# A 22nd weight slot in the routing's temporaries, and who waits for the first gather

## The chip, the cores and the metric

The kernel runs on one core of a Trainium2 chip. The metric is the device time of one execution in microseconds (us), less is better. "SP" is the engine that issues the weight loads, "POOL" is GpSimd, which issues gathers and scatters, "PE" is TensorE, "DVE" is VectorE and "ACT" is ScalarE. All of them run their own instruction streams and meet in semaphores.

## The reference, cut to what matters

The kernel computes one step of a two-layer encoder trunk on 512 prompt rows and 32 sample rows of 1024 floats. Each layer is an attention mixer followed by a mixture of experts (MoE) with 4 groups of 8 experts; a row goes to the two best experts of its best group:

```python
g_idx = jnp.argmax(pg, axis=-1)
...
top_v, top_i = lax.top_k(pe, TOP_K_IN_GROUP)
...
for g in range(N_GROUPS):
    a = jnp.einsum('nd,edf->nef', x, w_gate[g])
    u = jnp.einsum('nd,edf->nef', x, w_up[g])
    hh = jax.nn.silu(a) * u * gate[:, g, :, None].astype(x.dtype)
    y = y + jnp.einsum('nef,efd->nd', hh, w_down[g])
```

Each of the 32 experts has a gate, an up (1024 x 256) and a down matrix (256 x 1024), 1 MB each in float32, so a layer reads 96 MB of expert weights.

## The kernel before, in words

Attention and its projections run first. While the last output projections run, the rows are normed, turned, and routed: `logits`, `route_pick` and `route_place` find for each row its two experts and its place in them; `route_slots` multiplies a selection matrix (`sel`) with one-hot rows (`hot2`) and so makes, in PSUM, the list of rows of each expert. From it DVE makes the indices `idx_i` (L1425 to L1432), and POOL gathers the rows of two experts at a time from `hn_scratch` into `xg` (`gather`, L669). The rows are turned by `x_turn` (L2060).

Then 32 experts follow in order. For each: `gate_up` (L2075, L2076, 16 matmuls), ACT's SiLU (L966), DVE's product (L1475), `h_transpose` (L2082), `down` (L2087, L2088), DVE's copy (L1490), POOL's `scatter` to `y_scratch` (L675). TensorE does `gate_up(e)`, then `x_turn` after an odd e, `down(e - 1)`, `h_transpose(e)`. An expert has room for 64 rows. If one has more (`extra > 0`), an "overfull" expert is computed with the rest: picked after `OV_PICK`, listed after `OV_LIST`, its rows gathered by POOL at `OV_GATHER = 18`, and computed after expert `OV_AFTER` (L2125 turns its rows). With these inputs that happens once, in layer 1.

SP issues all weight loads in one order (`READ_ORDER`: gate and up of an expert, then down of the one before). They go round a ring of slots, `MOE_SLOTS`, of 2048 floats by 128 partitions. Six slots are the ring of the attention weights, the others are lent by tiles whose contents are over at some time; `vacant` says for what SP has to wait before a lent slot is first used in a layer. X0 and X1 lie in the turned rows of the routing, and H1 and H0 in `hid` itself, whose rows are read back from `hn_scratch` after the last use of each (L552). From the second turn on a load waits for the last use of the slot's former matrix (`load_after_owner`). The ring's slots R4, R5 and S0 are left out for one turn (`LEFT_OUT`) and take the three matrices of the overfull expert, which SP issues just before the load of `(OV_AFTER, 2)`.

Before H1, SP waits until the first gather of the layer has landed:

```python
if name == "H1":
    sp.wait_ge(gath[0], 16 * (TWOS // XG * layer + 1))
```

SP is in order, so H0 and all later loads are behind that wait.

After the last expert the rows are read back from `y_scratch`, weighted and added to `hid` (`combine`), and layer 1 or the final norm follows.

Of the kernel before, what the change touches and what calls it, by code (L numbers as in the profile page):

```python
# [21 lines left out]
ALU = mybir.AluOpType  # L22
# [3 lines left out]
D = 1024  # L26
SEQ, DEC, PAST = 512, 32, 256
CHUNK, WINDOW = 64, 128
N = SEQ + DEC
P = 128  # L30
KD = D // P
NT = 5
# [16 lines left out]
G, EPG, F = 4, 8, 256  # L49
NE = G * EPG  # L50
CAP = 64
MAX_EXTRA = 17
KEY0 = 2048
OUT_HALF = D // 2

SLOT = 2048
XG = 2
TWOS = NE // 2
OV_AFTER = 20
OV_PICK, OV_LIST, OV_GATHER = 14, 16, 18  # L60
assert OV_AFTER % 2 == OV_PICK % 2 == OV_LIST % 2 == 0

# [2 lines left out]
NL = 40  # L65
L_E = 8

UNITS = NT * 4
# [112 lines left out]

A_RING = ["R0", "R1", "R2", "R3", "R4", "R5"]
B_RING = ["R0", "R1", "R2", "R3", "R4", "R5"]
MOE_SLOTS = [["N0", "R4", "R5", "S0", "N1", "F5", "F6", "F0", "F1", "F2", "F3", "F4", "W0", "R0", "R1", "R2", "R3", "X0", "X1", "H1", "H0"]] * 2
NSLOT = len(MOE_SLOTS[0])


# [38 lines left out]
def program(nc, ctx, I, O):  # L226
# [3 lines left out]
    def sem(name):  # L230
        return ctx.enter_context(nc.semaphore(name))
# [6 lines left out]
    cst = sb("cst", [P, C_END])  # L238
# [5 lines left out]
    M0 = 7296  # L244
# [9 lines left out]
    def part(at, *shape):  # L254
        n = int(np.prod(shape))
        v = area[:, at:at + n]
        if len(shape) == 2:
            v = v.rearrange("p (a b) -> p a b", b=shape[1])
        if len(shape) == 3:
            v = v.rearrange("p (a b c) -> p a b c", b=shape[1], c=shape[2])  # L260
        return v

    slot_at = {f"R{i}": R_R + SLOT * i for i in range(6)}
    slot_at.update({f"F{i}": R_F + SLOT * i for i in range(7)})
    slot_at["S0"], slot_at["W0"] = R_S, 4864
    slot_at.update({f"N{i}": R_N + SLOT * i for i in range(2)})
    slot_at.update({f"X{i}": R_X + SLOT * i for i in range(2)})

# [55 lines left out]
    assert M1 + 1792 + 2 * 512 <= slot_at["W0"] and slot_at["W0"] + SLOT <= M0  # L324
    ovw = part(R_R + 4 * SLOT, 3, SLOT)
    y2b = [part(2 * D * i, 2, D) for i in range(3)] + [part(R_X + 2 * D * i, 2, D) for i in range(2)]
    assert 6 * D <= M0 and 4 * D <= KD * N


    stage_g, stage_e = part(M0, 2, KD, G), part(M0 + 64, 2, KD, NE)  # L330
    lg = part(M0, NT, NL)
    em = part(M0 + 200, NT, NE)

    hot2 = [part(M0 + 360 + 320 * i, NT, 2 * NE) for i in range(2)]
    hot = [h[:, :, 0:NE] for h in hot2]
    both = part(M0 + 1000, NT, NE)
    sofar = part(M0 + 1160, NT, NE)
    blocks = part(M0 + 1000, NE * 8)
    sel = [part(M0 + 1320 + 640 * i, NT, P) for i in range(2)]
    gtop, etop = part(M0 + 2600, NT, 8), part(M0 + 2640, NT, 8)  # L340
    chosen = part(M0 + 2680, NT, 4)
    where = part(M0 + 2700, NT, 2)
    pen = part(M0 + 2710, NT, G)
    rs = part(M0 + 2730, 12, 8)
    gexp = part(M0 + 2826, NT, G)
    gw = part(M0 + 2846, 2, 8)
    ovs = part(M0 + 2862, 128)
    shifted = part(M0 + 2990, NT, 2)
    root = part(M0 + 3000, NE)
    assert M0 + 3000 + NE <= R_G  # L350
    first_of = sb("first_of", [P, NT, 2, 8], U32)
    idx_i = sb("idx_i", [P, 3, NE], I32)
    ov_i = sb("ov_i", [P, 8], I32)
# [49 lines left out]
        sem("r_mm"), sem("r_exp"), sem("r_hot"), sem("r_before"), sem("r_sel"), sem("r_slots"), sem("r_idx"))  # L403
    r_d, r_sum = sem("r_d"), sem("r_sum")
    r_clear = sem("r_clear")
    ones = cst[:, C_ONE:C_ONE + P]
    before = cst[:, C_BEFORE:C_BEFORE + P]
    slot_no = cst[:, C_SLOT:C_SLOT + CAP].unsqueeze(1).broadcast_to([P, 2, CAP])
# [13 lines left out]
    def wait_apart(eng, s, value):  # L422

        eng.wait_ge(s, value)
        eng.sem_inc(passed, 1)
# [18 lines left out]
    def vacant(layer, name):  # L444

        c = "ab"[layer]
        if name in ("F5", "F6"):
            return [(pos_mm, len(POS))] if layer else [(q_mm, 16), (kv_mm, NT)]
        if layer and name in ("F0", "F1", "F2"):
            return [(at["b", "pv"], 15), (vb_out[0], 64)]  # L450
        if name[0] == "F":
            return [(at[c, "o"], UNITS)] + ([(vb_out[1], 64)] if layer else [(k_out, 16 * 6)])
        if name[0] == "N":
            return [(kb_out[0], 64), (kb_out[1], 64), (pos_mm, len(POS)), (made_once, 2)] if layer else [(y_flip, NT)]
        if name == "W0":
            return [(at[c, "o"], UNITS)]
        if name[0] == "X":
            return [(r_mm, NT * (layer + 1))]
        if name[0] == "H":
            return [(y_flip, NT * (2 * layer + 2)), (sumsq, NT * (2 * layer + 2))] + \  # L460
                [(y_out[b], 16 * (3, 2)[b] * (layer + 1)) for b in range(2)]
        return None
# [27 lines left out]
    def _(sp):  # L490
# [29 lines left out]
        def moe_loads(layer):  # L520
            s = ov[layer]

            def overfull_weights(o):
                wait_apart(sp, s["pick"], o + 1)
                e = sp.value_load(ov_u[0:1, 0:1], min_val=0, max_val=NE - 1)
                for j, w in enumerate((gate, up, down)):
                    src = w[layer][bass.ds(e, 1)].rearrange("o p k f -> p (o k) f")
                    sp.dma_start(ovw[:, j, :].rearrange("p (k f) -> p k f", f=src.shape[-1]), src) \
                      .then_inc(s["w"], 16)

            for n, (key, name) in enumerate(MOE_LOADS[layer]):
                if key[2:] == (OV_AFTER, 2):
                    for j in range(3):
                        sp.wait_ge(*last_use(("e", layer, *READ_ORDER[LEFT_OUT + j - NSLOT])))
                    sp.wait_ge(s["count"], layer + 1)
                    extra = sp.value_load(ov_i[0:1, layer:layer + 1], min_val=0, max_val=MAX_EXTRA)
                    with sp.If(extra > 0):
                        overfull_weights(0)
                free = vacant(layer, name) if expert_stream(*key[2:]) < NSLOT else None
                if free is None:  # L540
                    load_after_owner(key)
                else:
                    for signal in free:
                        sp.wait_ge(*signal)
                    if name == "H1":
                        sp.wait_ge(gath[0], 16 * (TWOS // XG * layer + 1))
                    load(key)

            for name in ("H1", "H0"):
                sp.wait_ge(*last_use([key for key, at in MOE_LOADS[layer] if at == name][-1]))  # L550
                for t in (2 * int(name[1]), 2 * int(name[1]) + 1):
                    sp.dma_start(hid[:, t, :], hn_dram[COL[t]:COL[t] + P, :]).then_inc(tile_in[t], 16)  # L552

            with sp.If(extra > 1):
                with sp.Fori(1, extra) as o:
                    overfull_weights(o)
# [29 lines left out]
    def _(pool):  # L586
# [77 lines left out]
        def moe(layer):  # L664
# [27 lines left out]
            for b in range(2):  # L692
                pool.wait_ge(y_out[b], 16 * (3, 2)[b] * (layer + 1))
            wait_apart(pool, r_idx, 2 * layer + 1)
            for j in range(XG):
                gather(j)
            pool.wait_ge(r_idx, 2 * layer + 2)
            for e in range(NE):
# [428 lines left out]
    def _(dve):  # L1127
# [175 lines left out]
        def moe(layer):  # L1303
# [122 lines left out]
            for b in range(2):  # L1426
# [1 line left out]
                ins = nc.vector.tensor_scalar(idx_i[rows, 1, 0:TWOS], idx_i[rows, 2, :].rearrange("p (j b) -> p b j", b=2)[:, b, :],  # L1428
                                              1, None, ALU.arith_shift_right)
            ins.then_inc(r_idx, 1)  # L1430
            own(dve, nc.vector.tensor_scalar(em[:, 0, :], ps[:, 3, 0:NE], -2.0, float(2 * KEY0), ALU.mult, ALU.add))
            nc.vector.tensor_scalar(idx_i[:, 0, :], em[:, 0, :], cst[:, C_HALF:C_HALF + 1], None, ALU.add) \  # L1432
                .then_inc(r_idx, 1)

            def per_tile(i):
# [78 lines left out]
            def overfull_select(o):  # L1514

                dve.wait_ge(s["mask"], o + 1)
                ins = nc.vector.tensor_copy(blocks[:, 0:NE], ps[:, 3, 0:NE])
                nc.vector.tensor_scalar(shifted[:, :, :], where[:, :, :], ps[:, 3, 64:65], None, ALU.subtract) \
                    .then_inc(s["seen"], 1)
                wait_apart(dve, s["seen"], o + 1)  # L1520
                for t in range(NT):
                    r = ROWS[t]
                    for c in range(2):
                        ins = nc.vector.tensor_scalar(sel[c][:r, t, :].rearrange("p (a b) -> p a b", b=CAP), slot_no[:r], shifted[:r, t, c:c + 1],
                                                      cst[:r, (C_K1, C_K2)[c] + t:(C_K1, C_K2)[c] + t + 1],
                                                      ALU.is_equal, ALU.mult)
                ins.then_inc(s["list"], 1)
# [51 lines left out]
            with dve.If(extra > 1):  # L1579
                with dve.Fori(1, extra) as o:  # L1580
                    overfull_pick(o)
                    overfull_select(o)
                    wait_apart(dve, s["scat"], 16 * o)
                    overfull_rows(o)
                    overfull_expert(o)

# [144 lines left out]
    def _(pe):  # L1731
# [316 lines left out]
        def moe(layer):  # L2048
# [63 lines left out]
            def overfull_list(o):  # L2112
                pe.wait_ge(s["list"], o + 1)
                for t in range(NT):
                    r = ROWS[t]
                    for c in range(2):
                        ins = nc.tensor.matmul(ps[:, 3, 0:2 * NE], sel[c][:r, t, :], hot2[c][:r, t, :],
                                               start=t == 0 and c == 0, stop=t == NT - 1 and c == 1)
                ins.then_inc(s["irow"], 1)

# [243 lines left out]
```

## Time and profile before

| | |
|---|---|
| three runs | 1138.3, 1138.5, 1140.09 us |
| profiled execution, its own time | 1136.48 us |
| its span in the trace | 1134.6 us |
| PE busy | 1009.6 us (89%) |
| DVE, ACT, POOL busy | 421.5, 231.9, 254.0 us |
| HBM read, over the span | 268.66 MB |
| the chain that ended last | PE 77%, DMA 13%, DVE 4% |
| weights' queue (q1) | 240.40 MB, 53.9% of the DMA engines' span |

The MoE of layer 0 runs from about 257 to 482 us, that of layer 1 from about 870 to 1104 us. The span is counted from the first instruction; the execution's own time also holds what lies around it. A busy PE is not PE at its peak, since matmuls are pipelined.

### The profile page before, as it was taken

What the parts mean: (1) busy time and instruction counts of PE and PEld (TensorE: products, weight loads), DVE (VectorE), ACT (ScalarE), POOL (GpSimd) and SP (SyncE); (2) the same over time, 40 slices, a digit from 0 to 9 for tenths busy, and PEclk for the clock granted to TensorE, in tenths of its full rate; (3) what the DMA queues carried; (4) which work ended last, traced back from release to release, by engine and by line L of the source; (5) the groups of instructions that cost most, each with busy time, mean ns of one, the idle gap of its engine ahead of it and who ended that gap; (6) DMA issues with size and microseconds to landing.
All of it is one profiled execution on the core that took longest, in us unless ns stands there. A gap on an engine that the chain in (4) does not pass through costs nothing.

```text
span 1134.6 us, 17373 instructions
## 1 busy us (share of the span) xinstructions
PE 1009.6 (89%) x6608; PEld 715.2 (63%) x6608; DVE 421.5 (37%) x1367; ACT 231.9 (20%) x717; POOL 254.0 (22%) x408
## 2 busy tenths in 40 slices
PE   6999999978999989839899899999996999888980
PEld 5877777965555545438668687777895555555540
DVE  1234454342333322241242433435464333432326
ACT  4234442110000000033222332332311000000002
POOL 3612232011222221122121221212211122221223
PEclk9999999978999999969999999999996999999995
DMA  9412141569999999993320402227066999999996
GB/s 314 124 40 75 39 186 64 217 244 336 416 419 417 416 420 418 392 317 126 119 80 27 134 31 94 66 102 290 24 258 237 382 419 417 418 418 419 418 372 243
DMA packets 73333, 282.12 MB, mean 249 GB/s; under 512 B 10410, under 2 KB 37114, under 8 KB 47200
## 3 DMA queue, kind: packets, MB, share of 16 engines
q1 hardware_dynamic: 57520, 240.40, 53.9%
q0 software_dynamic: 14480, 31.65, 8.0%
q10 hardware_dynamic: 1248, 8.91, 2.0%
q8 instruction: 56, 0.92, 0.3%
q14 instruction: 29, 0.24, 0.1%
HBM read 268.66 MB, written 28.70 MB: 262 GB/s over the span
## 4 chain that ended last, share of the span: by engine, by line
PE 77%; DMA 13%; DVE 4%; issue 2%; ACT 2%; POOL 1%; SPq 1%; POOLq 0%; ACTq 0%; DVEq 0%
PE ps L1773 22%; PE ps L2075 16%; PE ps L1765 11%; DMA area<-in_w_up 8%; PE ps L2087 7%; PE ps L2060 2%; PE ps L2266 2%; PE ps L1749 2%; PE ps L2082 2%; PE ps L1836 2%; PE ps L1958 1%; PE ps L2232 1%; PE ps L1973 1%; PE ps L1988 1%; DMA area<-y_scratch 1%
## 5 line engine op out<-in xcount | busy, mean ns | idle before, releaser
L1773 PE MATMUL ps<-area 128*128 128x256 f32 x1152 | 266.4, 384 | 7.1 <-DMA area<-in_w_b_qkv 3.3
L2076 PE MATMUL ps<-area 128*64 128x256 f32 x1040 | 251.8, 398 | 0.0
L1773 PEld LDWEIGHTS ps<-area 128*128 128x128 f32 x1152 | 214.0, 191 | 37.9 <-issue 8.2
L2075 PE MATMUL ps<-area 128*64 128x256 f32 x912 | 220.7, 397 | 14.7 <-DMA area<-in_w_up 7.7
L2075 PEld LDWEIGHTS ps<-area 128*64 128x64 f32 x912 | 125.5, 143 | 80.2 <-issue 21.1
L2076 PEld LDWEIGHTS ps<-area 128*64 128x64 f32 x1040 | 143.0, 143 | 0.0
L675 POOL DMA_INDIRECT y_scratch<-area,idx_i x64 | 63.8, 997 | 352.2 <-DVE area L1490 302.3
L1765 PE MATMUL ps<-area 128*128 128x272 f32 x512 | 123.2, 395 | 0.0
L1475 DVE SCALAR_TENSOR_TENSOR area<-ps,area 64x256 f32<-64x256 f32 x64 | 31.4, 491 | 232.4 <-ACT area L966 232.4
L966 ACT ACTIVATE area<-ps,area 64x256 f32<-64x256 f32 x64 | 29.9, 468 | 412.5 <-PE ps L2076 412.5
L2087 PE MATMUL ps<-area 128*64 128x512 f32 x228 | 108.7, 599 | 1.1 <-DVE area L1483 0.8
L2088 PE MATMUL ps<-area 128*64 128x512 f32 x228 | 108.7, 599 | 0.0
L1765 PEld LDWEIGHTS ps<-area 128*128 128x128 f32 x512 | 95.0, 190 | 18.9 <-issue 0.6
L931 ACT ACTIVATE area<-area,small 128x256 f32<-128x256 f32 (+5 forms) x160 | 80.2, 502 | 87.1 <-DVE small L1232 87.1
L1225 DVE CUSTOM_DVE_ANT_0 area<-ps,area 128x256 f32<-128x256 f32 (+5 forms) x160 | 59.1, 423 | 44.9 <-PE ps L1958 25.2
L793 POOL TENSOR_SCALAR area<-area,small 32x288 f32<-32x288 f32 (+4 forms) x40 | 20.5, 521 | 162.1 <-DVE small L1661 162.1
L2082 PEld LDWEIGHTS ps<-cst,area 64*128 64x128 f32 x130 | 20.2, 203 | 55.1 <-issue 53.6
L2087 PEld LDWEIGHTS ps<-area 128*64 128x64 f32 x228 | 28.7, 136 | 41.0 <-issue 32.4
L660 POOL TENSOR_SCALAR area<-area,small 128x256 f32<-128x256 f32 (+2 forms) x80 | 33.7, 439 | 92.5 <-DVE small L1260 92.5
L1470 DVE TENSOR_TENSOR area<-ps,gT 128x512 f32<-128x512 f32 x65 | 44.9, 691 | 13.8 <-PE ps L2060 7.6
L2060 PE MATMUL ps<-cst,area 128*128 128x128 f32 x256 | 38.7, 296 | 11.7 <-DMA area<-hn_scratch,idx_i 11.7
L2060 PEld LDWEIGHTS ps<-cst,area 128*128 128x128 f32 x256 | 32.3, 196 | 23.6 <-issue 17.7
(235 smaller groups left out, 1163.6 us busy)
## 6 DMA issues: line engine op xcount, KB each, us to landing
area<-in_w_up SPq DMA_DIRECT2D x65, 1024.0 KB, 24.6
area<-in_w_gate SPq DMA_DIRECT2D x57, 1024.0 KB, 23.0
area<-in_w_down SPq DMA_DIRECT2D x57, 1024.0 KB, 27.4
area<-in_w_b_qkv SPq DMA_DIRECT2D x12, 1024.0 KB, 8.5
hid<-in_w_down SPq DMA_DIRECT2D x8, 1024.0 KB, 24.5
hid<-in_w_gate SPq DMA_DIRECT2D x8, 1024.0 KB, 20.8
area<-y_scratch ACTq DMA_DIRECT2D x8, 1024.0 KB, 8.1
area<-in_w_a_qkv SPq DMA_DIRECT2D x6, 1024.0 KB, 13.0
```

Source lines behind the costliest of these rows:

```text
L675: nc.gpsimd.indirect_dma_start(y2_dram, bass.IndirectOffsetOnAxis(ap=idx_i[:, 0, e:e + 1], axis=0), yout[e % 2], None, bounds_check=4 * N ...
L931: ins = nc.scalar.activation(E[:r, g, 0:nk], E[:r, g, 0:nk], ACT.Exp, bias=sm[:r, 4 + g:5 + g], scale=SCALE, accum_out=sm[:r, 8 + g:9 + g])
L1225: ins = nc.vector.tensor_tensor_reduce(out=E[:r, g, 0:nk], in0=ps[:r, b, c:c + nk], in1=tab(j, g)[:r, tc:tc + nk], scale=1.0, scalar=-3e38 ...
L1470: return nc.vector.tensor_tensor(x, turned, gT[:, layer, :].unsqueeze(2).broadcast_to([P, KD, CAP]), ALU.mult)
L1765: ins = nc.tensor.matmul(ps[:, bank, 0:HALF_N], w[:, k, m * P:m * P + P], x[:, k, HALF_N * h:HALF_N * h + HALF_N], start=k == 0, stop=k == ...
L1773: ins = nc.tensor.matmul(ps[:r, bank, at_col:at_col + F], x[:, k, COL[t]:COL[t] + r], w[:, k, :], start=k == k0, stop=k == k1 - 1)
L2060: ins = nc.tensor.transpose(ps[:, 2 + k // 4, k % 4 * P:k % 4 * P + P], x[:, k, :], ident)
L2075: nc.tensor.matmul(ps[0:CAP, bank, 0:F], x[:, k, :], wg[:, k, :], start=k == 0, stop=k == KD - 1)
L2076: ins = nc.tensor.matmul(ps[CAP:P, bank, 0:F], x[:, k, :], wu[:, k, :], start=k == 0, stop=k == KD - 1)
L2082: ins = nc.tensor.transpose(ps[:, bank, c * CAP:c * CAP + CAP], rows[:, c, :], ident[CAP:P, CAP:P])
L2087: nc.tensor.matmul(ps[0:CAP, bank, :], ht[:, c, :], wd[:, c, 0:OUT_HALF], start=c == 0, stop=c == 1)
L2088: ins = nc.tensor.matmul(ps[CAP:P, bank, :], ht[:, c, :], wd[:, c, OUT_HALF:D], start=c == 0, stop=c == 1)
```

## The change

The routing's temporaries, which filled one stretch from M0 on, are laid out anew: those that are dead once the row lists stand in PSUM (`sel`, `both`, `sofar`, `em`) lie together, and a slot M of 2048 floats at 6960 covers them. The others (`hot2`, `lg`, `gtop`, `root`, ...) lie behind it; `idx_f` takes the place of `em` for the scatter's indices, `blocks` goes to the end of the turned rows' region, and the selection of the overfull expert gets tiles of its own (`ov_sel`). The ring has 22 slots, in another order: N1, F5 and F6 come before R4, R5, S0, and M stands between H1 and H0. `OV_AFTER` is 22, which keeps the left-out turn on R4, R5 and S0.

H1 waits no longer for the first gather. M waits for the last attention output, for the row lists (`r_slots`) and for a new semaphore `asked`, which POOL raises when it has issued gather 0. H0 is behind M in SP's order.

```diff
-OV_AFTER = 20
+OV_AFTER = 22
...
-MOE_SLOTS = [["N0", "R4", "R5", "S0", "N1", "F5", "F6", "F0", "F1", "F2", "F3", "F4", "W0", "R0", "R1", "R2", "R3", "X0", "X1", "H1", "H0"]] * 2
+MOE_SLOTS = [["N0", "N1", "F5", "F6", "R4", "R5", "S0", "F0", "F1", "F2", "F3", "F4", "W0", "R0", "R1", "R2", "R3", "X0", "X1", "H1", "M", "H0"]] * 2
...
-    slot_at["S0"], slot_at["W0"] = R_S, 4864
+    slot_at["S0"], slot_at["W0"], slot_at["M"] = R_S, 4864, 6960
...
+    R_T = 7232
+    sel = [part(R_T + 640 * i, NT, P) for i in range(2)]
+    both, sofar, em = (part(R_T + 1280 + 160 * i, NT, NE) for i in range(3))
+    stage_g, stage_e = part(R_T, 2, KD, G), part(R_T + 64, 2, KD, NE)
+    R_P = slot_at["M"] + SLOT
...
+    hot2 = [part(R_P + 320 * i, NT, 2 * NE) for i in range(2)]
...
+    idx_f = part(R_P + 1272, NE)
+    blocks = part(R_X + 2 * SLOT, NE * 8)
...
+    ov_at = [R_G + P * i for i in range(8)] + [R_F + 7 * SLOT + P * i for i in range(2)]
+    ov_sel = [[part(ov_at[NT * c + t], P) for t in range(NT)] for c in range(2)]
...
+    asked = sem("asked")
...
+        if name == "M":
+            return [(at[c, "o"], UNITS), (r_slots, layer + 1)]
...
-                    if name == "H1":
-                        sp.wait_ge(gath[0], 16 * (TWOS // XG * layer + 1))
+                    if name == "M":
+                        sp.wait_ge(asked, layer + 1)
                     load(key)
...
-            for j in range(XG):
+            gather(0)
+            pool.sem_inc(asked, 1)
+            for j in range(1, XG):
                 gather(j)
...
-            own(dve, nc.vector.tensor_scalar(em[:, 0, :], ps[:, 3, 0:NE], -2.0, float(2 * KEY0), ALU.mult, ALU.add))
-            nc.vector.tensor_scalar(idx_i[:, 0, :], em[:, 0, :], cst[:, C_HALF:C_HALF + 1], None, ALU.add) \
+            own(dve, nc.vector.tensor_scalar(idx_f, ps[:, 3, 0:NE], -2.0, float(2 * KEY0), ALU.mult, ALU.add))
+            nc.vector.tensor_scalar(idx_i[:, 0, :], idx_f, cst[:, C_HALF:C_HALF + 1], None, ALU.add) \
                 .then_inc(r_idx, 1)
...
-                        ins = nc.vector.tensor_scalar(sel[c][:r, t, :].rearrange("p (a b) -> p a b", b=CAP), slot_no[:r], shifted[:r, t, c:c + 1],
+                        ins = nc.vector.tensor_scalar(ov_sel[c][t][:r, :].rearrange("p (a b) -> p a b", b=CAP), slot_no[:r], shifted[:r, t, c:c + 1],
...
-                        ins = nc.tensor.matmul(ps[:, 3, 0:2 * NE], sel[c][:r, t, :], hot2[c][:r, t, :],
+                        ins = nc.tensor.matmul(ps[:, 3, 0:2 * NE], ov_sel[c][t][:r, :], hot2[c][:r, t, :],
```

## Rows read from the trace of the kernel before

**Rows 1.** Waits of TensorE, 257 to 480 us: us in total, times, longest

```profile
PE ps L2075 <- DMA area<-in_w_up: 10.2, 7, 2.5
PE ps L2060 <- DMA area<-hn_scratch,idx_i: 5.7, 1, 5.7
```

**Rows 2.** ScalarE's timeline, layer 0: SiLU of experts 0, 22 and 31 (start, us)

```profile
265.53 0.47 ACT L966 ACTIVATE area<-ps,area 64x256 f32<-64x256 f32 x1 [10.81 <-PE ps L2076]
...
404.92 0.47 ACT L966 ACTIVATE area<-ps,area 64x256 f32<-64x256 f32 x1 [6.47 <-PE ps L2076]
...
476.74 0.47 ACT L966 ACTIVATE area<-ps,area 64x256 f32<-64x256 f32 x1 [6.51 <-PE ps L2076]
```

**Rows 3.** TensorE's timeline: start, us; in brackets idle before it and releaser

```profile
473.02 0.40 PE L2075 MATMUL ps<-area 128*64 128x256 f32 x1 [1.22 <-DMA area<-in_w_up]
...
1018.89 1.06 PE L2125 MATMUL ps<-cst,area 64*128 64x64 f32 x8 [2.26 <-DMA area<-hn_scratch,ov_i]
...
1020.74 0.43 PE L2075 MATMUL ps<-area 128*64 128x256 f32 x1 [0.78 <-DVE area L1470]
...
1094.50 0.43 PE L2075 MATMUL ps<-area 128*64 128x256 f32 x1
```

**Rows 4.** Windows: PE, PEld, DVE, ACT, POOL busy; then PEclk, DMA share, GB/s

```profile
252.00:253.00 1.00, 0.00 (x0) 0.00 (x0) 0.89 (x8) 0.00 (x0) 0.00 (x0) 0.50 0.00 0
...
866.00:867.00 1.00, 0.00 (x0) 0.00 (x0) 0.87 (x6) 1.00 (x1) 1.00 (x1) 0.50 0.08 33
...
265.00:472.00 207.00, 195.95 (x1388) 111.87 (x1384) 62.76 (x122) 14.49 (x31) 42.58 (x42) 0.98 1.01 412
879.00:1090.00 211.00, 200.06 (x1426) 114.03 (x1426) 69.06 (x152) 14.49 (x31) 43.55 (x43) 0.98 1.01 413
...
257.00:263.00 6.00, 4.86 (x22) 3.29 (x24) 0.69 (x1) 0.00 (x0) 1.00 (x1) 0.50 0.86 308
870.00:878.00 8.00, 7.14 (x34) 4.44 (x36) 0.69 (x1) 0.00 (x0) 0.99 (x1) 0.50 0.83 317
```

**Rows 5.** Waits of SP's queue, whole span: us in total, times, longest

```profile
SPq L546 <- DMA area<-hn_scratch,idx_i: 20.9, 2, 11.2
```

**Rows 6.** SP's timeline: the issue of H1 in layer 0 and in layer 1

```profile
257.33 0.33 SPq L513 DMA_DIRECT2D hid<-in_w_down  x1
...
869.96 0.33 SPq L513 DMA_DIRECT2D hid<-in_w_down  x1
```

**Rows 7.** Single transfers: gathers of 253.3, 260.1, 283.3 and 296.1; load of 245.2

```profile
L669 POOL DMA_INDIRECT area<-hn_scratch,idx_i x1: 1312/1312/1312, 253.3 to 253.3; - x1
...
DMA to landing us min/median/max: 4.0/4.0/4.0
...
L669 POOL DMA_INDIRECT area<-hn_scratch,idx_i x1: 1002/1002/1002, 260.1 to 260.1; - x1
...
DMA to landing us min/median/max: 6.2/6.2/6.2
...
L669 POOL DMA_INDIRECT area<-hn_scratch,idx_i x2: 1048/1050/1052, 283.3 to 296.1; - x2
...
DMA to landing us min/median/max: 9.3/9.3/9.3
...
L513 SPq DMA_DIRECT2D area<-in_w_gate x1: 328/328/328, 245.2 to 245.2; - x1
...
DMA to landing us min/median/max: 5.0/5.0/5.0
```

**Rows 8.** Line L528: loads of the overfull expert, issue ns, start, us to landing

```profile
L528 SPq DMA_DIRECT2D area<-in_w_down x1: 2327/2327/2327, 981.0 to 981.0; - x1
...
DMA to landing us min/median/max: 26.5/28.8/29.3
```

**Rows 9.** Line L513, 1064.5 to 1065: the last up matrix of layer 1

```profile
L513 SPq DMA_DIRECT2D area<-in_w_up x1: 2642/2642/2642, 1064.5 to 1064.5; - x1
...
DMA to landing us min/median/max: 28.8/28.8/28.8
```

## What the change is expected to do

> **What bounds the kernel now.** I read the waits of TensorE first, then ScalarE's timeline (its one SiLU for each expert, L966, follows that expert's gate and up matmuls, so it is a clock of the experts), then the busy shares of the DMA engines, then the two DMA queues around the start of each MoE stage, because the change touches only what is loaded there.
>
> In the MoE stage of layer 0 TensorE sets the pace at first: the SiLU of expert 0 starts at 265.53 and that of expert 22 at 404.92 [rows 2], 139.39 / 22 = 6.34 us an expert. At that pace expert 31 would come at 404.92 + 9 x 6.34 = 462.0. It comes at 476.74 [rows 2], 14.7 us later. The reader is to see why: TensorE waits for an up matrix seven times [rows 1], and the last expert starts at 473.02 when its own up matrix lands [rows 3]. From 265 to 472 the DMA engines are full, share 1.01 at 412 GB/s [rows 4]. So the end of layer 0's MoE is the end of a stream of bytes that runs without a gap from about 265; TensorE falls into it near expert 23.
>
> In layer 1 the engines are as full (1.01 at 413 GB/s [rows 4]), but TensorE loses time on an overfull expert, which is computed after expert 20, and so is never caught by the weights. The margin at the end is thin: the last up matrix is issued at 1064.51 and takes 28.8 us [rows 9], so it is there at 1093.3, and expert 31 starts at 1094.50 [rows 3], 1.2 us later. Inside the overfull expert TensorE stands 2.26 us for the gather of its rows [rows 3]. So layer 1 is bound by TensorE's own order plus that wait, with the stream right behind.
>
> Ahead of both stages there is a hole in the DMA time. SP holds H1 back until the first gather has landed; the two waits sum to 20.9 us, the longer 11.2 [rows 5], so the other is 9.7. H1 is issued at 257.33 and at 869.96 [rows 6]; without the wait it would go at 257.33 - 9.7 = 247.6 and 869.96 - 11.2 = 858.8. From 252 to 253 the engines move nothing, and from 866 to 867 their share is 0.08 [rows 4].
>
> **The change, part by part.**
>
> *A 22nd slot.* Each layer loads 96 matrices of 1.05 MB (128 x 2048 floats). Those that find a lent slot free go before expert 0 is done; the rest are in the saturated stream. With 22 slots 74 are left for it in place of 75. H1 moves into the hole, M takes H1's place behind it. One load less is 1.05 MB / 412 GB/s = 2.55 us [rows 4]. In layer 0 that goes whole into the end, since the last up matrix releases the last expert: -2.55. It is far from being used up: the lateness there is 14.7 us. In layer 1 nobody waits for the stream, so by itself it is worth nothing and adds 2.55 to the margin of 1.2.
>
> *The overfull expert after expert 22 and not 20.* Its own work and its DMAs stay as many; its place in the streams of TensorE, ScalarE, VectorE and POOL is two experts later, 2 x 6.34 = 12.7 us. The gather of its rows keeps its place at expert 18. It lands at 1018.89 at the latest [rows 3], and is now wanted at about 1018.89 - 2.26 + 12.7 = 1029.3. So the wait goes: -2.26 in layer 1, nothing in layer 0, where this work is not entered. What is late next? Its three matrices. They now stand in SP's order before load 70 and not before load 64, so six more loads are ahead of them and, by the 22nd slot, one less: 5 x 2.55 = 12.8 us later. The third one is issued at 980.96 and the three take up to 29.3 us [rows 8], so it lands by 1010.3; it would land by 1023.1. TensorE wanted them at 1020.74 [rows 3] and will at 1020.74 - 2.26 + 12.7 = 1031.2. Eight us are over. Before these loads SP now waits for expert 17's gate matmuls, with everything in SP's queue behind it; that is some 7 us of waiting, while the loads already issued cover 28.8 us [rows 9]. So no engine runs dry. Then TensorE's gain of 2.26 has to fit the stream: 1.2 + 2.55 - 2.26 leaves 1.5 us. It fits.
>
> *H1 earlier.* Its bytes follow X1's in the same queue. In layer 0 they are through well before the gather at 253.3 brings its first ones. In layer 1 it is closer: H1 leaves at 858.8 behind X0 and X1, the engines are nearly idle from 866 on [rows 4], and 2.55 us more end at 868.5 at the latest, a us or so before the gather that H1 used to wait for landed, at about 869.9 [rows 6]. So it can run beside that gather's first bytes; this is in the bounds below.
>
> *M behind the first gather, not behind its landing.* POOL spends 1.31 us on the gather that starts at 253.3 and it lands after 4.0 [rows 7]. `asked` comes with the end of that instruction, so M leaves at about 254.7, H0 right behind. A lone 1.05 MB load takes 5.0 us to land [rows 7], of which its bytes are 2.55; so M's bytes cannot be there much before the gather's last ones. The first gather of each layer is on the path: TensorE stood 5.7 us for it [rows 1], and every us it lands later is a us on both the start of TensorE and the start of the stream. No row has a first gather beside a load, so bounds: below, 0; above, 2.2 a layer, because the gather of 260.1, issued with H1 and H0 in flight, takes 6.2 against 4.0 [rows 7]; farther still 5.3, because in the full stream a gather takes 9.3 [rows 7]. I take 0.3 a layer, near the lower end, as M starts 1.4 us behind. A gain is excluded, since before the gather had the engines to itself.
>
> By the row of 260.1 a load beside a gather costs that gather 2.2 us. The Trainium skill's page "DMA: Bandwidth & Descriptors", section "Queues, rings and completion order", says each DMA engine takes turns, a packet at a time, between the queues that have work, so SP's weights would not wait behind POOL's gather but take every other turn. That speaks against lending the engines to M before the gather is in; by it, with full overlap, the gather's half MB would take twice its 1.3 us, and the sum below would come to -2.3. The rows of 4.0 and 6.2 agree with it in kind.
>
> *The rest.* The temporaries at new addresses, the separate list tiles for the overfull expert, `idx_f`: the same instructions with the same shapes, 0. One semaphore increment on POOL between gathers 0 and 1, whose second is wanted ten us later, and one more wait on SP: 0. The lent slots H1 and H0 are used one expert longer, so the reload of `hid` waits one expert longer; its packets are behind some 28 us of issued loads and stay there: 0. The new order of the first slots moves loads that end long before they are read: 0.
>
> **The sum** against the profiled execution's 1136.48 us (span 1134.6): -2.55 - 2.26 + 0.3 + 0.3 = -4.2, so 1132.3. The median of the runs is 2.0 higher, at 1138.5; with the same difference, 1134.3.
>
> One more term has a width and no sign: TensorE's granted clock is 0.50, that is 1.2 GHz, from 257 to 263 in layer 0 and from 870 to 878 in layer 1 [rows 4], after it stood for the gather. The two stretches differ by 2 us, worth 1 us of work at half rate. A shifted start may land on either: up to 1 us each way and layer.
>
> **The rivals.** A change within 0.2% (2.3 us) is about what a measurement of this kernel can't tell from none.
>
> 1. *The forecast*, -4.2: 1134.3, own range 1132.7 to 1135.9 (on one side -4.8 with both gathers undisturbed and a us of clock; on the other half of the 2.2 a layer). Chance 0.68.
> 2. *The gathers share with the weights in full*, 2.2 each: -4.8 + 4.4 = -0.4, 1138.1. For it is the gather of 260.1; against it the head start of 1.4 us. Chance 0.13.
> 3. *A wait in the place of the removed one in layer 1* (the overfull expert's matrices or the stream): only layer 0 gains, -2.55 + 0.3 = -2.25, 1136.2. Against it are the 8 us and the 1.5 us above. Chance 0.09.
> 4. *Slower*: H1's tail, M and H0 together treat the first gather as the full stream treats any, 9.3 in place of 4.0: -4.8 + 10.6 = +5.8, 1144.3. It decides from 2.4 us of delay a layer. Against it, at 254.7 only one load's bytes can be near. Chance 0.06.
> 5. *The slot does nothing*, because slots and not bytes limit layer 0's stream: the overfull term and the delays stay, -2.26 + 0.6 = -1.7, 1136.8. The share of 1.01 speaks against it. Chance 0.04.
>
> Faster by over 0.2%: case 1 nearly whole and half of case 3, 0.71. Within: case 2, the other half of 3, case 5, and a little of 1, 0.21. Slower: case 4 and the clock's bad side on case 2, 0.08. The range runs from the forecast's low end with a second us of clock to case 2 with one on its bad side, and leaves out case 4: 1131.5 to 1139.0.
>
> **What the profile after would show.** H1's issue near 247.6 and 858.8 minus the shift; M's some 1.4 us after the gather's start. First gathers landing after 4.0 to 4.6 us: above 6 is case 2 or 4. The last up matrix of layer 0, counted from expert 0's SiLU, 2.55 us sooner, with TensorE still waiting there. No wait at L2125 before the overfull expert, and none for its weights. If expert 31 in layer 1 waits for `in_w_up`, the margin was wrong. What would make the total wrong: a late first gather, or a longer stretch at the low clock in either stage.

## The result and the profile after

The changed kernel takes 1147.65 us (median of four runs, 1147.15 to 1149.63), the kernel before 1138.56 beside it; the ratio is 1.0075, 95% interval 1.0054 to 1.0096. It is 9.1 us slower where 4.2 less was forecast. The profiled execution took 1147.15 us, its span is 1145.3, against 1136.48 and 1134.6 before.

TensorE's waits in the changed kernel, first from 250 to 500 us, then from 860 to 1130 us (us in total, times, longest; line 2070 was 2060, 2085 was 2075):

```profile
PE ps L2070 <- DMA area<-hn_scratch,idx_i: 12.4, 1, 12.4
PE ps L2085 <- DMA area<-in_w_up: 8.8, 5, 2.8
...
PE ps L2070 <- DMA area<-hn_scratch,idx_i: 11.1, 1, 11.1
```

The wait for the first gather was 5.7 us in layer 0 [rows 1] and 6.0 in layer 1; it is 12.4 and 11.1 now. The gather itself shows why. Its own line in each layer, and how long it took to land:

```profile
L677 POOL DMA_INDIRECT area<-hn_scratch,idx_i x1: 1313/1313/1313, 252.9 to 252.9; - x1
...
DMA to landing us min/median/max: 10.6/10.6/10.6
...
L677 POOL DMA_INDIRECT area<-hn_scratch,idx_i x1: 1395/1395/1395, 869.8 to 869.8; - x1
...
DMA to landing us min/median/max: 9.3/9.3/9.3
```

It lands after 10.6 and 9.3 us; before it was 4.0 [rows 7] and, in layer 1, 4.2. And the timeline of all engines around it, in layer 0:

```profile
252.72 0.33 SPq L521 DMA_DIRECT2D area<-in_w_gate  x1
...
252.86 1.31 POOL L677 DMA_INDIRECT area<-hn_scratch,idx_i  x1 [9.82 <-DVE idx_i L1442]
...
253.22 0.33 SPq L521 DMA_DIRECT2D hid<-in_w_up  x1
```

SP issues M at 252.72, that is 0.14 us *before* POOL's engine begins the gather, and H0 at 253.22, while the engine is still at work on it (1.31 us). The forecast had M at 1.4 us behind the gather's start. So 2.1 MB of weights are in the queues before the gather's first row is. H1, now free, is not out of the way either: issued at 246.05, it lands 9.3 us later, 2.5 us after the gather's start, and the DMA engines stand at a share of 0.99 where they moved nothing before [rows 4]:

```profile
252.00:253.00 1.00, 0.00 (x0) 0.00 (x0) 0.91 (x6) 0.32 (x2) 0.14 (x1) 0.50 0.99 418
```

ScalarE's SiLUs, the clock of the experts (experts 0, 22, 31 of layer 0, then 0, 22, the overfull one, 23 and 31 of layer 1):

```profile
272.42 0.47 ACT L976 ACTIVATE area<-ps,area 64x256 f32<-64x256 f32 x1 [18.13 <-PE ps L2086]
...
411.85 0.47 ACT L976 ACTIVATE area<-ps,area 64x256 f32<-64x256 f32 x1 [6.47 <-PE ps L2086]
...
480.56 0.47 ACT L976 ACTIVATE area<-ps,area 64x256 f32<-64x256 f32 x1 [6.20 <-PE ps L2086]
...
887.46 0.47 ACT L976 ACTIVATE area<-ps,area 64x256 f32<-64x256 f32 x1 [16.20 <-PE ps L2086]
...
1035.23 0.47 ACT L976 ACTIVATE area<-ps,area 64x256 f32<-64x256 f32 x1 [6.47 <-PE ps L2086]
1046.85 0.47 ACT L981 ACTIVATE area<-ps,area 64x256 f32<-64x256 f32 x1 [11.15 <-PE ps L2086]
1058.41 0.47 ACT L976 ACTIVATE area<-ps,area 64x256 f32<-64x256 f32 x1 [11.10 <-PE ps L2086]
...
1108.99 0.47 ACT L976 ACTIVATE area<-ps,area 64x256 f32<-64x256 f32 x1 [5.23 <-PE ps L2086]
```

This gives the ledger. Expert 0 of layer 0 is 6.89 us later than at 265.53 [rows 2]. From expert 0 to 31 it takes 208.14 us, 3.07 less than before (476.74 - 265.53 = 211.21 [rows 2]). From there to expert 0 of layer 1 it takes 406.90 against 402.32 (expert 0 of layer 1 was at 879.06 before): 4.58 more, of which the second late gather is 5.1. Inside layer 1 it takes 221.53 against 219.16, 2.37 more; that was forecast as 2.26 less. The end is 0.07 shorter. 6.89 - 3.07 + 4.58 + 2.37 - 0.07 = 10.7, the difference of the spans. Against the forecast's -4.2 that is 14.9 us too much: 11.1 for the two gathers (11.7 measured, 0.6 forecast) and 5.0 for the step around the overfull expert, treated next; the slot gave 0.5 more than forecast, and all the rest took 0.7 less.

The loss inside layer 1 is in the step around the overfull expert: 23.18 us from expert 22 to 23 (1035.23 to 1058.41). Before it was 20.43, from expert 20 (1014.58) to 21 (1035.01). The windows of the changed kernel there (sixth column PEclk, the granted share of TensorE's clock):

```profile
1041.00:1044.00 3.00, 3.00 (x16) 1.66 (x14) 0.00 (x0) 0.00 (x0) 0.39 (x1) 0.50 0.99 414
...
1047.00:1050.00 3.00, 1.63 (x8) 0.67 (x10) 0.78 (x2) 0.32 (x1) 0.00 (x0) 0.90 1.00 410
1050.00:1052.00 2.00, 1.91 (x6) 0.23 (x2) 0.05 (x1) 0.00 (x0) 0.00 (x0) 0.50 1.04 434
...
1054.00:1056.00 2.00, 2.00 (x12) 1.23 (x10) 0.00 (x0) 0.00 (x0) 0.00 (x0) 0.50 1.02 426
```

and the same part in the kernel before:

```profile
1021.00:1024.00 3.00, 3.00 (x18) 1.72 (x16) 0.00 (x0) 0.00 (x0) 0.00 (x0) 0.55 1.02 423
1024.00:1027.00 3.00, 2.10 (x16) 1.05 (x12) 0.29 (x1) 0.47 (x1) 0.00 (x0) 0.88 1.03 410
1027.00:1031.00 4.00, 2.36 (x10) 0.80 (x10) 1.18 (x3) 0.00 (x0) 0.00 (x0) 1.00 1.02 422
```

The reader is to see one short fall to 1.2 GHz before, and two long ones after. In windows of 1 us the granted clock is at 0.50 for some 3.4 us from 1021.3 on before, and for some 6.8 us each from 1039.4 and from 1049.4 on after; each fall comes behind a stretch in which TensorE stood part of the time.

The wait at L2135 (L2125 before) for the overfull expert's gather is gone, as forecast. But TensorE still stands there, for DVE's copy of the expert before:

```profile
1038.35 1.11 PE L2135 MATMUL ps<-cst,area 64*128 64x64 f32 x8 [1.07 <-DVE area L1500]
```

This wait of 1.07 us was there before as well, hidden under the one of 2.26: TensorE stood from 1016.63 (1018.89 - 2.26) and DVE's copy ended at 1017.56. So the move could give 2.26 - 1.07 = 1.2 us and not 2.26. Two things were to be tested: what the early loads cost, and what the clock does.

### The profile page after: what moved, and what is told of

Read it like the earlier page. It is cut to its first block, busy times and chain, and to the rows that moved or that the text cites. A ratio compares the mean times of both kernels' runs of the same rounds, so it can differ in the third digit from the quotient of the medians.

```text
span 1145.3 us, 17377 instructions
## 1 busy us (share of the span) xinstructions
PE 1010.7 (88%) x6608; PEld 714.2 (62%) x6608; DVE 421.8 (37%) x1367; ACT 231.9 (20%) x717; POOL 254.4 (22%) x408
## 4 chain that ended last, share of the span: by engine, by line
PE 81%; DMA 10%; DVE 4%; issue 2%; ACT 2%; POOL 1%; SPq 0%; ACTq 0%; POOLq 0%; DVEq 0%
PE ps L1783 22%; PE ps L2085 18%; PE ps L1775 10%; PE ps L2097 9%; DMA area<-in_w_up 5%; PE ps L2070 3%; PE ps L2276 2%; PE ps L2092 2%; DMA area<-hn_scratch,idx_i 2%; PE ps L1759 2%; PE ps L1846 1%; PE ps L1968 1%; PE ps L2242 1%; PE ps L1983 1%; PE ps L1998 1%
## 5 line engine op out<-in xcount | busy, mean ns | idle before, releaser
L2085 PE MATMUL ps<-area 128*64 128x256 f32 x976 | 237.5, 399 | 17.2 <-DMA area<-in_w_up 8.8
L2086 PE MATMUL ps<-area 128*64 128x256 f32 x944 | 230.3, 400 | 0.0
L2085 PEld LDWEIGHTS ps<-area 128*64 128x64 f32 x976 | 135.0, 143 | 89.9 <-issue 26.7
L2097 PE MATMUL ps<-area 128*64 128x512 f32 x236 | 113.7, 604 | 1.1 <-DVE area L1493 0.8
L2098 PE MATMUL ps<-area 128*64 128x512 f32 x236 | 113.6, 604 | 0.0
```

What stands on the lines that cost most here:

```text
L2085: nc.tensor.matmul(ps[0:CAP, bank, 0:F], x[:, k, :], wg[:, k, :], start=k == 0, stop=k == KD - 1)
L2086: ins = nc.tensor.matmul(ps[CAP:P, bank, 0:F], x[:, k, :], wu[:, k, :], start=k == 0, stop=k == KD - 1)
L2097: nc.tensor.matmul(ps[0:CAP, bank, :], ht[:, c, :], wd[:, c, 0:OUT_HALF], start=c == 0, stop=c == 1)
L2098: ins = nc.tensor.matmul(ps[CAP:P, bank, :], ht[:, c, :], wd[:, c, OUT_HALF:D], start=c == 0, stop=c == 1)
```

## The experiments

**1 to 4. Order against place.** Each differs by a few lines from the changed kernel, the second from the one before. The cuts show the lines on which each rests. Kernel 2 also gets the increment of `asked` behind gather 0; in 1, 6, 7 and 9 to 12 nobody waits for `asked`, and the increment is taken out.

```diff
 # 1: m_after_landing (the changed kernel, M and H0 behind the landing)
-                        sp.wait_ge(asked, layer + 1)
+                        sp.wait_ge(gath[0], 16 * (TWOS // XG * layer + 1))
 # 2: before_with_asked (the kernel before, H1 and H0 wait for asked)
-                        sp.wait_ge(gath[0], 16 * (TWOS // XG * layer + 1))
+                        sp.wait_ge(asked, layer + 1)
 # 3: asked_by_engine (the changed kernel)
-            pool.sem_inc(asked, 1)
+            nc.gpsimd.memset(small[:, 52:53], 0.0).then_inc(asked, 1)
 # 4: h0_after_landing (the changed kernel)
+                    if name == "H0":
+                        sp.wait_ge(gath[0], 16 * (TWOS // XG * layer + 1))
```

> The changed kernel, but M (and H0 behind it) waits until the first gather has landed, as H1 did before. Theory A (in the changed kernel the loads of M and H0 are issued before POOL's engine has begun the gather, so their bytes are ahead of it): the first gathers land 4.0 to 4.3 us after their start again, expert 0's SiLU comes at about 265 in layer 0, and what the extra slot and the later overfull expert bring is seen: about 1134 to 1137 us, under the kernel before. Theory B (the new ring or the overfull expert's new place costs the time): first gathers as fast as before, but the time stays over 1140.

> The kernel before with one thing changed: H1, and H0 behind it, waits for the new semaphore that POOL raises behind gather 0, not for its landing. 21 slots, overfull expert after expert 20. Theory A: first gathers land after 9 to 11 us, TensorE's wait for them grows by 5 to 7 us in each layer, and nothing gives it back but the DMA time gained in layer 0: 1146 to 1151 us. Theory B: no change, 1138 to 1140.

> The changed kernel, but the semaphore is raised by a tiny memset on POOL's engine behind gather 0, which can start only when the engine has built the gather's descriptors (1.3 to 1.4 us). Theory A, order is what matters: M is issued about 1.5 us after the gather's start, the first gathers land after 4.0 to 4.6, total 1134 to 1137. Theory C, sharing is what matters, whatever the order: the first gathers land after 6 us or more, total 1138 to 1142.

> The changed kernel, but H0 waits for the landing of the first gather, so one load (M) is issued ahead of it and not two. Theory A: each load ahead costs the gather its 2.5 us of bytes, so it lands after about 7 to 8 us in place of 10.6 and 9.3: total about 1141 to 1144. Theory C with equal turns from the start of the gather: one load in place of two makes little difference while it lasts, 9 to 10 us and about 1147.

Measured, each against runs of the kernel before on the same chip; "first gathers" is the landing time in layer 0 and 1, "layer 0" from SiLU 0 to 31 in the profiled execution, "overfull step" the distance of the two SiLUs around it. The last three columns come from one profiled execution of each kernel:

| kernel | ratio to before, 95% interval | first gathers | layer 0 | overfull step |
|---|---|---|---|---|
| before | 1 | 4.0, 4.2 | 211.2 | 20.4 |
| changed | 1.0075, 1.0054 to 1.0096 | 10.6, 9.3 | 208.1 | 23.2 |
| 1, M and H0 after landing | 0.9986, 0.9969 to 1.0002 | 4.0, 5.8 | 208.4 | 23.2 |
| 2, before with `asked` | 1.0060, 1.0042 to 1.0079 | 8.3, 8.4 | 211.6 | 20.6 |
| 3, `asked` by the engine | 1.0002, 0.9980 to 1.0024 | 4.1, 8.6 | 208.3 | 23.2 |
| 4, H0 after landing | 1.0041, 1.0022 to 1.0060 | 5.6, 8.0 | 208.4 | 19.0 |

Kernel 2 has neither the new slot nor the moved expert, and loses 0.6% by the semaphore alone: theory A in kind, theory B falls. Kernel 1 undoes the early loads and is back at the time of before. In layer 0 more bytes ahead mean a later gather: 4.0 us with no early load, 5.6 with one behind H1, 8.3 with two (kernel 2, whose H1 is one of the two), 10.6 with two behind H1. In kernel 2 the DMA engines moved nothing from 253 to 254; in the changed kernel H1's last bytes were still going, which accounts in kind for 10.6 in place of 8.3. Kernel 3 splits the two theories by layer. In layer 0 it is enough that M comes behind the gather's start, here 1.5 us behind, at 254.79; the gather is in after 4.1 us:

```profile
253.27 1.31 POOL L677 DMA_INDIRECT area<-hn_scratch,idx_i  x1 [9.47 <-DVE idx_i L1442]
254.59 0.12 POOL L704 MEMSET small<- 128x1 f32 x1
254.79 0.33 SPq L521 DMA_DIRECT2D area<-in_w_gate  x1
```

The DMA engines were full of H1 when this gather began, but had room again before M came:

```profile
253.00:254.00 1.00, 0.00 (x0) 0.00 (x0) 0.90 (x5) 0.90 (x3) 0.73 (x1) 0.50 1.03 426
254.00:255.00 1.00, 0.00 (x0) 0.00 (x0) 0.87 (x6) 0.70 (x1) 0.81 (x3) 0.50 0.53 221
```

In layer 1 that is not enough: M comes as late (866.41 against 864.81), yet the gather takes 8.6 us. H1 is still on its way there: it lands 3.7 us after the gather's start (3.1 in layer 0), and the share is 0.98 from 864 to 866 and 0.83 from 866 to 868. H1 alone (kernels 1, 11 and 8) makes it 5.8, 5.0 and 5.2, where it lands 4.8, 4.1 and 3.9 us after the gather's start; in layer 0 (kernels 1, 3, 6, 8 and 11) it lands after 2.2 to 3.9 us and the gather after 3.8 to 4.6, the later the later. So theory C holds in layer 1: there the gather pays also for what comes behind it. That H1's remainder is what makes the difference between the layers is read from these rows; no run varied it alone. Kernel 4's gather of layer 0 is faster than expected, 5.6 for 7 to 8 us, and its median 1144.6 where 1141 to 1144 was expected. The totals of 1 and 3 missed their expectation, 1134 to 1137 us: they were 1138.0 and 1140.4 beside 1140.0 of before. The step around the overfull expert accounts for part of it, and H1 for another, as the next runs show.

**5 to 8. The parts one by one.**

```diff
 # 5: overfull_later_alone (the kernel before, 21 slots)
-OV_AFTER = 20
+OV_AFTER = 22
-MOE_SLOTS = [["N0", "R4", "R5", "S0", "N1", "F5", "F6", "F0", "F1", "F2", "F3", ...
+MOE_SLOTS = [["N0", "N1", "F5", "F6", "F0", "F1", "F2", "R4", "R5", "S0", "F3", ...
 # 6: m_both_h1_layer0 (the changed kernel)
-                    if name == "M":
-                        sp.wait_ge(asked, layer + 1)
+                    if name == ("M", "H1")[layer]:
+                        sp.wait_ge(gath[0], 16 * (TWOS // XG * layer + 1))
 # 7: slot_alone_h1_waits (the changed kernel)
-                    if name == "M":
-                        sp.wait_ge(asked, layer + 1)
+                    if name == "H1":
+                        sp.wait_ge(gath[0], 16 * (TWOS // XG * layer + 1))
 # 8: h1_free_alone (the kernel before)
-                    if name == "H1":
+                    if name == "H0":
```

> The kernel before with only the overfull expert moved behind expert 22 (21 slots; R4, R5 and S0 stand eighth to tenth in the ring so that the left-out turn fits). The prediction's step: its wait of 2.26 us for its gather is gone, the step around it takes 18.2 us and the kernel about 2.3 us less than before. Theory D, from the runs so far (23.2 us around it in three traces with it behind expert 22, 19.0 in one, 20.4 and 20.6 behind expert 20): without that wait TensorE's granted clock falls for longer inside it, 23 us around it and the kernel 2 to 3 us slower than before. Theory E: where the clock falls is chance, so the median is between the two.

> The changed kernel, but M waits for the first gather's landing in layer 0 and H1 does so in layer 1 (so H1 uses the idle DMA time in layer 0 alone). Theory A with what the earlier run showed of H1's tail beside layer 1's gather: first gathers land after 4.0 and 4.2 us, layer 0 from expert 0 to 31 takes 208.3 us (211.2 before), 1.6 us less than with H1 free in both. Kernel 1 to 3 us under before.

> The changed kernel with H1 waiting for the first gather's landing in both layers, as before; M and H0 behind it. The prediction's step says the slot gives 2.55 us because H1 moves into idle DMA time; with H1, M and H0 all behind the landing there are three loads in front of the ring's first refill, so layer 0 from expert 0 to 31 takes 210 to 211 us, 1 us or less under before. If it takes 208.3, the slot gives its time without the hole.

> The kernel before with the wait for the first gather moved from H1 to H0, nothing else (21 slots). Theory A: layer 0's gather still 4.0 us, layer 1's 5 to 6 us because H1's bytes are still going; layer 0's stream gains at most the 1 us in which the engines stood still before the first refill. Total 0 to 1.5 us over before.

| kernel | ratio to before, 95% interval | first gathers | layer 0 | overfull step |
|---|---|---|---|---|
| 5, overfull later alone | 0.9982, 0.9964 to 1.0000 | 4.1, 4.4 | 213.2 | 19.1 |
| 6, H1 free in layer 0 | 0.9946, 0.9928 to 0.9963 | 4.6, 4.4 | 211.4 | 19.1 |
| 7, H1, M, H0 after landing | 0.9955, 0.9936 to 0.9974 | 3.8, 4.1 | 208.7 | 19.0 |
| 8, H1 free alone | 0.9994, 0.9976 to 1.0013 | 3.8, 5.2 | 212.9 | 22.2 |

Kernel 7 is the changed one with the old wait, and is 0.45% *faster* than the kernel before; my expectation that the slot would then bring 1 us or less was wrong. Layer 0 takes 208.7, so the slot gives its time without the idle stretch ahead of the gather. There is room behind it, as the same kernel run again (12, below) shows. The first two rows are kernel 12, the third is the kernel before:

```profile
262.00:266.00 4.00, 4.00 (x22) 2.30 (x20) 0.00 (x0) 0.00 (x0) 0.00 (x0) 0.50 1.01 420
266.00:270.00 4.00, 2.62 (x24) 1.50 (x22) 1.38 (x3) 0.47 (x1) 0.00 (x0) 0.99 0.86 334
...
265.00:270.00 5.00, 3.63 (x34) 2.17 (x32) 1.38 (x3) 0.47 (x1) 0.00 (x0) 1.00 0.75 255
```

Kernel 12 has 0.90 from 265 to 270, and 0.99 from 264 to 266 where the kernel before has 0.47.

H1, M and H0, 2.5 us each from some 2 us after 257.4, are nearly done when expert 0 opens the ring's first refill at 266.8. Kernel 8 says the same from the other side: H1 in the idle stretch brings nothing by itself and makes layer 1's gather take 5.2. Kernel 5 has the forecast direction, 0.18% where 2.3 us (0.20%) was forecast, at the edge of what its interval can tell.

Kernel 6 missed its expectation twice: layer 0 took 211.4 and not 208.3, and yet it is 5.6 us under before where 1 to 3 was expected. Its trace is not typical: the profiled execution took 1138.52, one of four at 1137.3 to 1138.7, while the other eight lie at 1131.9 to 1134.0. Its layer 0 is long although its overfull step is short, so the two vary apart. Over all fourteen traces experts 0 to 22 of layer 0 take 139.4 us, whatever the kernel; the differences arise between expert 22 and 31, where TensorE waits for the weights: 71.8 to 73.7 us with 21 slots (four traces), 68.7 to 69.8 with 22 (nine traces), and 72.0 in kernel 6. That is about 3 us for the slot with a scatter of 1 to 2, and why kernel 6's trace stands out was not tried.

**9 to 12. Why the overfull step is 19 or 23 us.** Kernels 9 and 10 are kernel 7 with layer 1's first gather held back by 8 or 16 tiny memsets on POOL; 11 is kernel 1 and 12 is kernel 7 again.

```diff
             wait_apart(pool, r_idx, 2 * layer + 1)
+            for _ in range(8 * layer):
+                own(pool, nc.gpsimd.memset(small[:, 52:53], 0.0))
             gather(0)
```

> The 22-slot kernel with H1, M and H0 behind the landing (the fastest kind so far), and 8 tiny memsets on POOL before layer 1's first gather, so that layer 1's experts start about 1.7 us later, as late as with H1 free, but with no load beside the gather. Theory F (how long the granted clock stays low around the overfull expert depends on when TensorE starts, not on what the loads do): the step from expert 22 to 23 takes 23.2 us in some runs and the median is more than 1.7 us over the same kernel without the memsets, up to 1.7 + 4. Theory G (the loads beside it matter): 19.0 us around it as in the kernel without them, median 1.7 us over.

> The same with 16 memsets, about 3.4 us later. Theory F: again other than the plain 3.4 us over, by up to 4 us either way. Theory G: 3.4 us over and 19.0 us around the overfull expert.

> The changed kernel with M and H0 behind the landing and H1 free in both layers, a second time, beside the one with H1 waiting too. If the first measurement holds, it is 3 to 5 us over that one: 1.6 of it the later gather of layer 1, the rest a 23.2 us step around the overfull expert in place of 19.0 in most runs.

> The 22-slot kernel with H1, M and H0 behind the landing in both layers, a second time: 0.4 to 0.5% under the kernel before, first gathers 3.8 to 4.2 us, 19.0 us around the overfull expert.

The first gathers of the two layers take 4.0 and 4.0 us in kernel 9, 4.1 and 4.2 in 10, 4.4 and 5.0 in 11, 4.0 and 4.2 in 12.

| kernel | median, us (before: 1139.59) | ratio to before, 95% interval | overfull step |
|---|---|---|---|
| 9, 8 memsets | 1138.19 | 0.9983, 0.9966 to 1.0000 | 23.2 |
| 10, 16 memsets | 1137.59 | 0.9975, 0.9955 to 0.9994 | 19.2 |
| 11, M and H0 after landing | 1137.31 | 0.9976, 0.9957 to 0.9995 | 23.2 |
| 12, H1, M, H0 after landing | 1133.46 | 0.9948, 0.9932 to 0.9964 | 19.1 |

The memsets were cheaper than I had reckoned, 1.7 and 3.4 us: TensorE waits for layer 1's first gather for 7.04 us in kernel 9 and 8.67 in kernel 10, against 5.96 in kernel 12 and 5.92 in 7, so its start is 1.1 and 2.7 us later. (Counted from the start of the span the first `x_turn` of kernel 9 is only half a us behind kernel 12's, 869.22 against 868.69, since everything ahead of it happened to be earlier in that execution.) In kernel 9 the profiled step grew from 19.1 to 23.2 and the median by 4.7 for 1.1 us of delay. No load is beside the gather in either. So theory F says it rightly for kernel 9 and G, with 19.0 us and 1.7 over, does not. Kernel 10 does not tell them apart: its step is 19.2 and its median 4.1 over kernel 12, where G had 3.4 and F up to 4 us to either side of that. Kernel 11 is 3.9 over kernel 12, as expected. The SiLUs of kernel 9 (expert 22, the overfull one, 23), then of kernel 12:

```profile
1025.73 0.47 ACT L977 ACTIVATE area<-ps,area 64x256 f32<-64x256 f32 x1 [6.47 <-PE ps L2087]
1037.41 0.47 ACT L982 ACTIVATE area<-ps,area 64x256 f32<-64x256 f32 x1 [11.21 <-PE ps L2087]
1048.97 0.47 ACT L977 ACTIVATE area<-ps,area 64x256 f32<-64x256 f32 x1 [11.09 <-PE ps L2087]
```

```profile
1026.19 0.47 ACT L975 ACTIVATE area<-ps,area 64x256 f32<-64x256 f32 x1 [6.47 <-PE ps L2085]
1036.36 0.47 ACT L980 ACTIVATE area<-ps,area 64x256 f32<-64x256 f32 x1 [9.70 <-PE ps L2085]
1045.29 0.47 ACT L975 ACTIVATE area<-ps,area 64x256 f32<-64x256 f32 x1 [8.47 <-PE ps L2085]
```

and their windows, kernel 9 then 12:

```profile
1029.00:1037.00 8.00, 7.22 (x40) 4.24 (x40) 0.69 (x1) 0.00 (x0) 2.04 (x2) 0.57 1.02 422
...
1039.00:1046.00 7.00, 5.31 (x20) 2.10 (x22) 0.98 (x2) 0.00 (x0) 0.00 (x0) 0.58 1.01 422
```

```profile
1030.00:1033.50 3.50, 2.72 (x16) 1.63 (x17) 0.69 (x1) 0.00 (x0) 2.03 (x2) 0.59 1.02 424
1033.50:1037.00 3.50, 2.75 (x24) 1.46 (x20) 0.14 (x1) 0.47 (x1) 0.00 (x0) 0.92 1.00 416
1037.00:1041.00 4.00, 2.36 (x10) 0.80 (x10) 1.33 (x3) 0.00 (x0) 0.00 (x0) 1.00 1.03 421
```

The clock falls twice for long in one and once for short in the other, under the same work. What goes with it is visible 160 us earlier. From layer 1's first `x_turn` to the first matmul at full rate it took 6.26, 6.25, 6.64, 7.07 and 7.06 us in the traces of the changed kernel, 1, 3, 9 and 11, and all five have the 23.2 us step; it took 7.82, 7.94, 8.37, 8.29, 8.74 and 8.81 in 4, 7, 12, 6, 5 and 10, and all six have 19.0 to 19.2. With the overfull expert behind expert 20 there are only three traces, and this mark does not sort them: 7.96 us and a step of 20.4 in the kernel before, 7.50 and 20.6 in kernel 2, each with one fall, but 7.94 and 22.2 in kernel 8, with two short ones. So the mark is a finding of one arrangement, made after the runs, and not a rule.

Timed runs scatter alike: the twelve of kernel 12 lie between 1132.7 and 1137.5, nine of the twelve of kernel 11 at 1136.2 to 1139.4, two at 1133.0 and one at 1141.6. That the longer times are the executions with the long falls is read from these clusters, not from a trace of each; kernel 6, whose traced execution is a long one with a short step, shows that the falls are not the only cause. The traced execution of kernel 4 is the shortest of its ten, 1139.17 with a median of 1144.62, so its step of 19.0 need not be its usual one.

## Why the prediction was wrong, point by point

**The step that failed** is "`asked` comes with the end of that instruction, so M leaves at about 254.7". The increment is one of POOL's instruction stream and not of the engine behind it, and it passed while the engine had not begun: M left 0.14 us ahead of the gather's start in layer 0 and in layer 1 as well (869.64 and 869.78). I read 1.31 us off the gather's row [rows 7] and took it for the time after which the queue goes on. The price of +0.3 a layer was really +6.6 and +5.1, the growth of the gather's landing. Kernel 3, where the increment is the engine's own, shows M where I had put it, and 4.1 us in layer 0. The Trainium skill, page "DMA: Bandwidth & Descriptors", section "Anatomy of one DMA — SWDGE (gpsimd) path", lists the sequencer's dispatch and the generation of the descriptors as separate parts; the trace agrees in that SP's load, which waited for the increment, went 0.14 us ahead of the 1.31 us that the engine then spent on the gather.

**The bound was too low.** I took 2.2 a layer as the upper bound, from a gather with two loads in flight, and named 5.3 as farther; 6.6 is outside both. The gather of 260.1 started when part of the loads was through. One behind two full loads waits for nearly all their bytes, 5.1 us, and more. Case 4 had the place, "H1's tail, M and H0 together", with a chance of 0.06; its time of 1144.3 is 3.3 under the median measured, since the step around the overfull expert grew besides.

**H1's earlier issue** had no term of its own. In layer 1 it costs 0.8 to 1.6 (5.0, 5.2 and 5.8 against 4.2), for no gain: kernels 7 and 12 are as fast without it as any. I had H1's bytes follow X1's within 2.55 us; the load took 9.4 to 10.0 us to land there and was in 3.7 to 4.8 us after the gather's start. In layer 0 too, where I had it through well before, it landed 2.5 us after the start in the changed kernel.

**The slot's 2.55 us** was right in size, as far as the scatter lets one tell: layer 0 took 3.07 less in the changed kernel, 2.0 to 3.1 less in eight of the other nine with 22 slots, and 0.2 more in kernel 6. The reason, H1 in the idle stretch, was not needed: there was room behind the gather. That the size came out in spite of it is luck.

**The overfull expert** lost its wait for the gather, but the term of -2.26 was too large: under that wait lay one of 1.07 us for DVE's copy, which I did not look for, so 1.2 was to be had. Its weights were in time: they are issued at 1005.6 at the latest and land within 26.7 us, 1032.3, wanted at 1040.24, eight us over, as worked out. Where the clock falls once for short, the gain is 20.43 - 19.05 = 1.4, near that 1.2; where it falls twice for long the step is 2.8 longer than before. **The clock's width** of 1 us a layer was drawn from the start of the stages, and looked there alone. It was too narrow, 4.1 us in one step, in a place where I had priced no clock at all.

**The margin of layer 1's stream** held: nobody waited for `in_w_up` there.

With the step mended, in kernel 12, the time is 0.52% less than before (0.36 to 0.68), 5.9 us, against the 4.8 that the slot and the overfull expert make in the forecast. That these are near each other is in part luck: in its trace the slot gave 3.05 and the overfull step 1.3, 4.4 together. Kernels 6, 7 and 12 are the fastest, and their intervals overlap.

## What to carry to other kernels

An increment that stands by itself behind a DMA in GpSimd's stream says here that the DMA instruction was handed over, not that the engine has begun on it. If a transfer has to be first, wait for its landing, or let an instruction of the engine itself raise the semaphore. And ask first what the wait costs: here some 10 us of SP's waiting in each layer cost nothing (kernels 7 and 12), because the loads behind it were wanted much later.

Price a change of a few tenths of a percent against where the granted clock falls as well: shift TensorE's start by a us, and see whether the time moves by more than that. And before a wait is priced as a gain, look for the next one under it.

## What was not expected of the hardware

- POOL's increment after an indirect DMA was seen by SP, and SP's load issued, 0.14 us before the engine's own work on that DMA began; that work took 1.31 to 1.40 us.
- A first gather of 128 rows takes 3.8 to 4.4 us alone. In layer 0 it takes 5.6 with one load of 1 MB issued just ahead, and 8.3 and 10.6 with two, one of them just ahead and one 0.4 us behind its start. On busy DMA engines in layer 1 two loads issued 1.6 and 2.1 us behind its start still bring it to 8.6. The Trainium skill, page "DMA: Bandwidth & Descriptors", section "Queues, rings and completion order", has the engines take turns between queues; by turns alone, as an estimate from its half MB at 412 GB/s, the gather would take about 1.3 us more. With one load ahead the trace is near it, 1.6 more; with two it is not, 4.3 to 6.6 more. There the measurement decides: the gather fares much worse than every other turn.
- How long TensorE's clock stays at 1.2 GHz at a stage's start (6.3 to 8.8 us) goes with whether it falls once for short or twice for long 160 us later, in the eleven traces of eleven with the overfull expert behind expert 22. The three with it behind expert 20 do not follow it. What carries this over was not tried.
